# The long matmuls of a hybrid encoder take their columns in runs of sixteen, high and low parts by turns

## The reference

```python
def hybrid_layer(x, ...):
    hn = rms_norm(x, norm_w)
    u = einsum("bsd,dn->bsn", hn, w_in) + b_in          # 2048 -> 22544 columns
    q, k, v, o, z_a, gates, glu_a, glu_b, z_b, g_a, g_b = split(u)
    ...                                                  # conv, silu, bidirectional mLSTM, 4 heads
    y_a = einsum("bsw,wd->bsd", ya, w_a)
    c = depthwise_conv(glu_a * sigmoid(glu_b), dw_w) + dw_b
    c = silu(layer_norm(c, ln_w, ln_b)) * silu(z_b)
    y_b = einsum("bsw,wd->bsd", c, w_b)
    merged = sigmoid(g_a) * y_a + sigmoid(g_b) * y_b
    return x + einsum("bsd,de->bse", merged, w_out)
```

## Time and profile before

| | |
|---|---|
| median of 3 runs | 2401.4 us (2401.31 to 2402.68) |
| profiled execution | 2402.0 us |
| its span, first to last instruction | 2399.9 us |
| mean granted TensorE clock | 1.000 |
| TensorE busy, weight loads busy | 2388.9 us, 2101.8 us |
| VectorE, ScalarE, GpSimd busy | 1954.4 us, 1391.6 us, 73.0 us |
| read from HBM | 441.59 MB, 185 GB/s over the span |

### The profile page before, as it was taken

One profiled execution on the slowest core, in us unless ns is written; L12 is line 12 of the kernel. 1 busy time (PEld: TensorE's weight loads), 2 busy tenths in 40 slices (PEclk: granted clock), 3 DMA queues, 4 the chain that ended last, 5 costly groups with the idle time before them and its releaser, 6 DMA issues.

```text
span 2399.9 us, 38509 instructions
## 1 busy us (share of the span) xinstructions
PE 2388.9 (100%) x13966; PEld 2101.8 (88%) x13966; DVE 1954.4 (81%) x2991; ACT 1391.6 (58%) x1686; POOL 73.0 (3%) x42
## 2 busy tenths in 40 slices
PE   9999999999999999999999999999999999999998
PEld 7888888888888888888888888888888888888887
DVE  8898989898987877556678899999999887865565
ACT  7655564646465557555565655555555655665554
POOL 0000000000000000000000000000000000000000
PEclk9999999999999999999999999999999999999999
DMA  7676656566566666665656666665656666666654
GB/s 214 190 198 192 179 176 185 178 184 178 176 193 191 187 183 199 187 192 191 181 168 192 195 184 180 181 182 175 186 174 180 190 193 192 177 200 192 190 186 140
DMA packets 448714, 444.61 MB, mean 185 GB/s; under 512 B 18032, under 2 KB 445824, under 8 KB 448640
## 3 DMA queue, kind: packets, MB, share of 16 engines
q1 hardware_dynamic: 448640, 443.74, 62.0%
HBM read 441.59 MB, written 2.10 MB: 185 GB/s over the span
## 4 chain that ended last, share of the span: by engine, by line
PE 93%; DVE 4%; SPq 1%; ACT 1%; DMA 1%; issue 0%; ACTq 0%; DVEq 0%
PE ps L1576 55%; PE ps L1579 28%; PE ps L1594 4%; PE ps L1598 2%; DVE W L841 1%; DVE ACC L994 1%; DMA RAW<-in_w_in_dram 1%; SPq L345 0%; PE ps L1839 0%; ACT W L438 0%; DVE HEAD L1198 0%; PE px L1773 0%; PE px L1794 0%; PE px L1772 0%; PE px L1795 0%
## 5 line engine op out<-in xcount | busy, mean ns | idle before, releaser
L1576 PE MATMUL ps<-Hs,W 128*128 128x512 f32 x4928 | 1533.3, 392 | 0.4 <-DVE W L841 0.4
L841 DVE TENSOR_TENSOR W<-RAW,W 128x1024 fp32r<-128x1024 f32 x832 | 1008.9, 1220 | 370.2 <-ACT W L438 367.5
L438 ACT CAST W<-RAW 128x1024 fp32r<-128x1024 f32 x832 | 862.3, 1049 | 699.3 <-PE ps L1579 598.2
L1579 PEld LDWEIGHTS ps<-Hs,W 128*128 128x128 f32 x4928 | 925.4, 188 | 204.5
L1579 PE MATMUL ps<-Hs,W 128*128 128x256 f32 x4928 | 972.8, 279 | 0.0
L1576 PEld LDWEIGHTS ps<-Hs,W 128*128 128x128 f32 x4928 | 747.5, 188 | 2.5 <-issue 1.5
L994 DVE SCALAR_TENSOR_TENSOR ACC<-CP,CWT,ACC 128x256 f32<-128x256 f32 x928 | 404.5, 495 | 0.2
L1576 PE MATMUL ps<-YC,W 128*128 128x512 f32 x1120 | 347.8, 392 | 0.0
L1579 PEld LDWEIGHTS ps<-YC,W 128*128 128x128 f32 x1120 | 210.3, 188 | 46.3
L1579 PE MATMUL ps<-YC,W 128*128 128x256 f32 x1120 | 221.0, 279 | 0.0
L1576 PEld LDWEIGHTS ps<-YC,W 128*128 128x128 f32 x1120 | 169.7, 188 | 0.2
(11 more groups left out here) (234 smaller groups left out, 1183.7 us busy)
## 6 DMA issues: line engine op xcount, KB each, us to landing
RAW<-in_w_in_dram SPq DMA_DIRECT2D x640, 512.0 KB, 3.7
RAW<-in_w_a_dram SPq DMA_DIRECT2D x64, 512.0 KB, 3.4
RAW<-in_w_b_dram SPq DMA_DIRECT2D x64, 512.0 KB, 3.3
RAW<-in_w_out_dram SPq DMA_DIRECT2D x64, 512.0 KB, 4.1
M<-in_x_dram SPq DMA_DIRECT2D x4, 512.0 KB, 7.3
HEAD<-in_b_in_dram SPq DMA_DIRECT2D x8, 256.0 KB, 4.7
out_dram<-M SPq DMA_DIRECT2D x4, 256.0 KB, 3.2
out_dram<-M SPq DMA_DIRECT2D x2, 512.0 KB, 4.8
```

Of the source, the lines that this page charges most:

```text
L438: nc.scalar.copy(WH[:, c, :, :], RAW[:, c, :, :]).then_inc(hi_made, 1)
L841: v.tensor_tensor(WL[:, c, :, :], RAW[:, c, :, :], WH[:, c, :, :].bitcast(F32), ALU.subtract).then_inc(lo_made, 1)
L1576: mm(ps[:, 2 * q + t, :], WH[:, c, kk, t * P:t * P + P], act_in[:, kt, :], start=(kt == 0), stop=False)
L1579: i = mm(ps[:, 2 * q + t, S:2 * S], WL[:, c, kk, t * P:t * P + P], act_in[:, kt, 0:S], start=False, stop=(kt == KT - 1))
```

## The change

A helper permutes a range of 512 columns, seen as 2 halves (a) of 16 groups (b) of 16 columns (c): it walks the groups in order and takes in each the sixteen of the first half, then the sixteen of the second. Both the streamed input and the output of the long matmuls in `multiply` go through it. So the columns stream as 0-15, 256-271, 16-31, 272-287 and so on, and each result is written to the place it had before. The instructions, their number, their order and their waits stay as they are.

```diff
+
+        def by_turns(columns):
+
+            return columns.rearrange("p (a b c) -> p b a c", a=2, c=16)
...
                         for t in range(2):
-                            mm(ps[:, 2 * q + t, :], WH[:, c, kk, t * P:t * P + P], act_in[:, kt, :],
-                               start=(kt == 0), stop=False)
+                            mm(by_turns(ps[:, 2 * q + t, :]), WH[:, c, kk, t * P:t * P + P],
+                               by_turns(act_in[:, kt, :]), start=(kt == 0), stop=False)
```

## The result

| | before | after |
|---|---|---|
| median | 2401.4 us | 2488.8 us (4 runs, 2488.67 to 2489.02) |
| ratio | | 1.0363, 95% interval 1.0351 to 1.0375 |
| profiled execution, span | 2402.0, 2399.9 us | 2488.9, 2486.8 us |
| TensorE, VectorE, ScalarE busy | 2388.9, 1954.4, 1391.6 us | 2477.0, 1964.3, 1394.3 us |

The kernel is 87.4 us slower, which is 14.5 ns for each of the 6048 long matmuls. The forecast, no difference, was wrong; of the rivals A had given 2480 us and B more.

A forecast was written before the change was run, and what follows sets the result against it. TensorE was taken to bound the kernel; 0 for instructions and waits, 0 for input and 0 for output, on the median of 2401.4 us, gave 2401.4 us (no difference, chance 0.53), range 2390 to 2490.

The forecast's parts named there:

- Rival A: Long matmuls: every break costs one tick on the read or write side, 12.9 ns each, 78 us, 2480 us; chance 0.22.
- rival B: Long matmuls' output: broken runs upset the read and write behind each addition, 157 to 1290 us, 2559 to 3691; chance 0.15.
- What bounds the kernel: Whole kernel: everybody waits for TensorE, so added time per long matmul reaches the end nearly in full, 6048 times.
- The step of the clock and the columns: Input-tile loop: 0.690 us per step, 1536 columns in 640 ns at one per tick, plus four fixed parts of about 12.5 ns.
- The output side, 0: Long matmuls' writes into PSUM with addition: 31 breaks taken to cost 0, though no trace row showed a broken write.
- The bound itself: Output writes: at the trace's slowest stream, two ticks per column, 213 ns more per long matmul, 1290 us.
- The input side, 0: Long matmuls' reads from SBUF: 31 breaks, 1 KB on and nearly 1 KB back, taken to cost 0 each.
- The backward read of the earlier trace: Gate sort's backward input against its forward one: reading against the grain costs at most 10 ns in 256 columns.
- The turned products of the earlier trace: Matmuls streaming 512 columns from W in two runs of 256: 0.694 us per step, so 0 to 2 ns per break.
- The upper end: Long matmuls' input: 31 breaks at 2 ns, 62 ns per long matmul, 375 us in all.
- A's signs: Expected profile: second long start 13 ns later, step 0.716 us, short and turned matmuls keep spacing, ScalarE waits about 78 us more.
- Rival C: Long matmuls: fixed part between matmuls shrinks or a weight-load conflict eases, 5 ns each, 30 us, 2371 us; chance 0.10.

The follow-up runs named there:

- half-pace kernel: Changed kernel with long matmuls in plain fp32, two ticks per column, the first of each two in plain order, the second by turns on both sides: 6207.4 us.

## Why the prediction was wrong

**What bounds the kernel: right.** TensorE set the end before and after, and what a step pays came through in full: 29.1 ns more in each of 3024 steps of the trace are 88 us, against 87.4 us in the medians.

**The step of the clock and the columns: right as far as it went.** 1536 ticks and 50 ns of fixed parts per step, at the same granted clock. "The stream itself already runs at one column per tick" was the key to the result, but it was used only to exclude a gain. It should also have led to the question whether this stream has as much time to spare as the ones that it was compared with.

**The output side, 0: right.** Measured 0.0 ns for 31 breaks (2401.13 against 2401.2 us). The range that was kept open for it, up to 1290 us, and with it rival B, had nothing in it. The bound itself misreads: the two lines call four plain fp32 matmuls each in the two layers and left eight rows each, so, as in the half-pace kernel, one such matmul is two passes and takes four ticks per column, not two. By the prediction's own rule the bound would have been 6048 x 0.640 = 3871 us.

**The input side, 0: this is the step that failed.** The prediction took "0 per break" since "a run of 16 has 15 regular steps for each jump, and both rows allow nothing". Neither row bears on 31 breaks at full pace. The backward read of the earlier trace rows is a plain fp32 one at two ticks per column; the half-pace kernel shows that there even the very pattern of the change is free, and backwards at full pace (read and write) costs 8.0 ns per 512 columns. The turned products of the earlier trace rows have one break, and the kernels with one and with seven breaks cost nothing; their extra 4 ns per step (2 ns as means of the whole trace, 694.0 against 692.0) must have another source, if the kernel of one break is a measure. What the runs show in place of the 0 is 14.5 ns per long matmul with the input alone broken, 2488.8 us. The upper end, 2 ns per break and 375 us, came from that same misread row and was four times too high for runs of 16.

**Rival A, one tick per break, 2480 us: right in size, not in law.** 12.9 ns were forecast and 14.5 measured, 0.47 ns per break instead of 0.42. But as a law it gives 18 us for 7 breaks (measured 0) and 159 us for 63 (measured 79.5). It named the argument that counted, 31 breaks against the one that the trace showed, and then gave more weight to a row at half pace. The range, to 2490, held the time only because A was in it, and with 1.2 us to spare: that is luck, since A's price per break is not what the other run lengths pay. Nor did the short matmuls keep their spacing, which A's signs had asked for (121.5 ns between the two, 116.7 before).

**Rival C, faster:** no kernel was faster; the best, 2401.05 us, is the plain one's time. No version beat the kernel before, so there is none to recommend.

## What to carry to other kernels

Before a row of the trace is taken as proof that some pattern is free, compare its ticks per column, its type and its number of breaks with those of the stream in question: here a pattern that was free at two ticks per column cost 14.5 ns at one. For fp32r matmuls of 512 columns fed from SBUF, keep the streamed operand in forward runs of 64 columns or more, the shortest that were free here; the output could be broken into runs of 16 at no cost.

## What the hardware showed that was not expected

- Broken input costs 14.5 ns for 31 breaks in 512 columns of fp32r at one tick each; in plain fp32 at two ticks each, with the same breaks, starts stay 0.43 us apart.
- The same 31 breaks in the output alone cost 0.0 ns (2401.13 against 2401.2 us).
- The cost doesn't rise steadily with the number of breaks: 63 breaks (13.2 ns) are cheaper than 31 (14.5 ns).
- Reading and writing backwards costs 8.0 ns per 512 columns, reading one column twice at each of 31 breaks 12.8 ns, and the distance between the two places, 32 or 256 columns, makes no difference (2488.71 and 2488.8 us).
- Runs of 2 cost 103.9 ns, four times as much as runs of 4. The Trainium skill, in "Advanced Engine Details and Errata", section SBUF Cachelines, has lines of 16 bytes and asks for at least two hits on one to absorb the latency of the memory. Runs of 2 have two hits and still pay about a tick each, but the output is broken there too and may have a part in it. Runs of 16 use every line whole, and with the input alone broken they cost 14.5 ns, so here the measurement decides: hits on a line don't settle what is free.
